# One feed-forward loop, reordered: two tiles' high-weight products first, then the low-weight products of both

## The chip, the cores and the metric

The kernel runs on one core of one Trainium2 chip. The metric is the device time of one launch in microseconds, the median of the runs shown. A core has five engines that run their own instruction streams and meet at semaphores: TensorE (PE) multiplies matrices and writes into eight PSUM banks, VectorE (DVE) and ScalarE (ACT) do elementwise work, GpSimd (POOL) does a little of it and starts transfers, SyncE (SP) starts transfers.

## The reference

Two decoder layers over 256 tokens of width 1024, in float32. Layer 0 mixes with sparse latent attention and stick-breaking attention, layer 1 with block-sparse attention. Behind each mixer stands a normalisation, a feed-forward part and a second normalisation. The change concerns only the feed-forward part:

```
def swiglu(x, w_gate, w_up, w_down):
    return (jax.nn.silu(x @ w_gate) * (x @ w_up)) @ w_down

h = layer_norm(DEEPNORM_ALPHA * h + m, ln_mix_g[i], ln_mix_b[i])
f = swiglu(h, ffn_gate[i], ffn_up[i], ffn_down[i])
h = layer_norm(DEEPNORM_ALPHA * h + f, ln_ffn_g[i], ln_ffn_b[i])
```

The hidden width of the feed-forward part is 2816, that is 22 tiles of 128 columns.

## The kernel before, in words

**Splitting the numbers.** PE multiplies in a shorter format (fp32r). To keep precision each float32 operand is split into a high part (`hi`, the value cast to fp32r) and a low part (`lo`, the rest), and a product is made as hi x hi + hi x lo + lo x hi. Weights arrive as float32 in 1 MB chunks in the buffer `raw` (two slots). ACT casts a chunk to `whi` (`split_hi`, line 376) and DVE subtracts to get `wlo` (`split_lo`, line 753), each in two halves of 128x1024. Both parts lie in the ring `wboth` of six chunks. A chunk is converted four chunks ahead of its use (`AHEAD`). This is the conversion of a chunk in what follows.

**The weight stream.** SP loads the chunks in a fixed order (line 295). It refills a half of a `raw` slot when DVE has done the low half of the chunk that lay there (`wlo_ready`). In the feed-forward loop three chunks make a step: one of `w_down` (two rows of tiles), then two of gate and up (one tile of each).

**PE in a step.** `down` (line 1618) multiplies two finished tiles by their rows of `w_down`: 24 products of 512 columns (line 1244), accumulated in banks 4 to 7 over the whole loop. `gate_up` (line 1607) makes one tile. Its high-weight products (`half_hi`, line 1152) take the high and low parts of the activations side by side as one moving operand of 512 columns: 8 products for gate into one bank, 8 for up into the next; these 16 are a *wide run*. Its low-weight products (`half_lo`, line 1158) have 256 columns and add to the first half of the same banks: 16 products, a *narrow run*. Even tiles use banks 2 and 3, odd ones 0 and 1 (`tile_bank`). Before its wide run a tile waits for its own chunk (`wlo_ready`) and for the sum of the tile two before, which frees the banks (`usum_ready`).

**Evacuation of a tile.** `ffn_tile` on ACT (lines 654 to 661) and on DVE (lines 1050 to 1061) take turns: ACT copies gate's second half out of the bank (L654, when `gate_done` comes from the first half of the narrow run), DVE adds the first half (L1050), ACT applies silu (L657) and copies up's second half (L659, when the tile's last product is done), DVE adds (L1053, this is the sum `usum`) and multiplies (L1058), ACT makes the high part (L661) and DVE the low part (L1061) for `down`.

**The order** is written out by hand on each engine. In `ffn`, two tiles and the start of the first rows stand before the loop; PE runs the first pass of the loop as straight code and three more in a hardware loop. A pass (`four_tiles`) has two steps, so there are eight steps in a layer. `ffn_tile` begins with the conversion of chunk `c + AHEAD`, so ACT's and DVE's order in a step was: conversion, conversion, evacuation, conversion, evacuation. Behind the loop come two single tiles, then the last three down chunks (`last_out`), among which the normalisation `norm` begins. `down` of a step uses the tiles of two pairs before.

Of the kernel before, what the change touches and what calls it, by code (L numbers as in the profile page):

```python
# [43 lines left out]
AHEAD = 4  # L44
# [16 lines left out]
def build(nc, x, xT, stream, w_uk, w_uv, kv_norm, ln_rows, consts, out):  # L61
    with ExitStack() as ctx:
# [207 lines left out]
        def tile_bank(t):  # L270

            return 2 * ((t + 1) % 2)
# [100 lines left out]
        def _(act):  # L373
# [273 lines left out]
            def ffn_tile(L, c, t, i=0, more=1, ahi_first=False):  # L647

                n = FT * L + t + 4 * i
                m = n + 1 - 2 * (L + 1)  # L650
                if more and not ahi_first:
                    split_hi(c + AHEAD, i)
                act.wait_ge(gate_done, m)
                nc.scalar.copy(gful[:, t % 2], bank[tile_bank(t)][:, S:2 * S]).then_inc(glo_ready, 1)  # L654
                act.wait_ge(gsum_ready, m)
                act.wait_ge(amul_ready, n - 1)
                nc.scalar.activation(sgate[:, t % 2], gful[:, t % 2], ACT.Silu).then_inc(silu_ready, 1)  # L657
                act.wait_ge(chunk_used, c + 1 + RING * i)
                nc.scalar.copy(uful[:, t % 2], bank[tile_bank(t) + 1][:, S:2 * S]).then_inc(ulo_ready, 1)  # L659
                act.wait_ge(amul_ready, n + 1)  # L660
                nc.scalar.copy(ahi[:, FF_SLOT[t], :], aful[:, t % 2]).then_inc(ahi_ready, 1)  # L661
                if more and ahi_first:
                    split_hi(c + AHEAD, i)

            def ffn(L):


                base = L0_FFN if L == 0 else L1_FFN
                ffn_rows(L, base)
                for t in (2, 3):  # L670
                    ffn_tile(L, base + t, t)
                with act.Fori(0, LOOPS) as i:
                    for j in range(2):
                        c = base + 4 + 3 * j
                        split_hi(c + AHEAD, i)
                        ffn_tile(L, c + 1, 4 + 2 * j, i)
                        ffn_tile(L, c + 2, 5 + 2 * j, i)
                c = base + 4 + RING * LOOPS
                for at in range(3):
                    more = c + at + AHEAD < CHUNKS  # L680
                    if at < 2:
                        ffn_tile(L, c + at, 4 + 4 * LOOPS + at, 0, more, at == 1)
                    elif more:
                        split_hi(c + at + AHEAD)
# [64 lines left out]
        def _(dve):  # L749
# [6 lines left out]
            def split_lo(c, i=0):  # L756

                for j in range(2):
                    split_lo_half(c, j, i)
# [284 lines left out]
            def ffn_tile(L, c, t, i=0, more=1, alo_first=False):  # L1044
                n = FT * L + t + 4 * i
                m = n + 1 - 2 * (L + 1)
                if more and not alo_first:
                    split_lo(c + AHEAD, i)
                dve.wait_ge(glo_ready, m)
                nc.vector.tensor_tensor(gful[:, t % 2], bank[tile_bank(t)][:, 0:S], gful[:, t % 2], ALU.add  # L1050
                                        ).then_inc(gsum_ready, 1)
                dve.wait_ge(ulo_ready, m)
                nc.vector.tensor_tensor(uful[:, t % 2], bank[tile_bank(t) + 1][:, 0:S], uful[:, t % 2], ALU.add  # L1053
                                        ).then_inc(usum_ready, 1)
                dve.wait_ge(silu_ready, n + 1)
                dve.wait_ge(usum_ready, m)
                dve.wait_ge(alo_ready, n - 1)
                nc.vector.tensor_tensor(aful[:, t % 2], sgate[:, t % 2], uful[:, t % 2], ALU.mult  # L1058
                                        ).then_inc(amul_ready, 1)
                dve.wait_ge(ahi_ready, n + 1)  # L1060
                nc.vector.tensor_tensor(alo[:, FF_SLOT[t], :], aful[:, t % 2], ahi[:, FF_SLOT[t], :].bitcast(F32),  # L1061
                                        ALU.subtract).then_inc(alo_ready, 1)
                if more and alo_first:
                    split_lo(c + AHEAD, i)

            def ffn(L):


                base = L0_FFN if L == 0 else L1_FFN
                ffn_rows(L, base)  # L1070
                for t in (2, 3):
                    ffn_tile(L, base + t, t)
                with dve.Fori(0, LOOPS) as i:
                    for j in range(2):
                        c = base + 4 + 3 * j
                        split_lo(c + AHEAD, i)
                        ffn_tile(L, c + 1, 4 + 2 * j, i)
                        ffn_tile(L, c + 2, 5 + 2 * j, i)
                c = base + 4 + RING * LOOPS
                for at in range(3):  # L1080
                    more = c + at + AHEAD < CHUNKS
                    if at < 2:
                        ffn_tile(L, c + at, 4 + 4 * LOOPS + at, 0, more, at == 1)
                    elif more:
                        split_lo(c + at + AHEAD)
# [44 lines left out]
        def _(pe):  # L1130
# [4 lines left out]
            def chunk(c, i=0):  # L1135
                pe.wait_ge(wlo_ready, 2 * c + 2 * RING * i)
# [12 lines left out]
            def half_hi(dst, slot, off):  # L1149

                for k in range(KT):
                    mm(dst[:], whi[:, slot, off + k * P:off + (k + 1) * P],  # L1152
                       hTs[:, k].rearrange("p j s -> p (j s)"), start=(k == 0), stop=False)

            def half_lo(dst, slot, off):

                for k in range(KT):
                    last = mm(dst[:, 0:S], wlo[:, slot, off + k * P:off + (k + 1) * P], hThi[:, k, :],  # L1158
                              start=False, stop=(k == KT - 1))
                return last  # L1160
# [443 lines left out]
                                               aful[:, tile, t * P:(t + 1) * P], ident)  # L1604
                last.then_inc(ff_turned, 1)

            def gate_up(L, c, t, i=0):

                n = FT * L + t + 4 * i
                chunk(c, i)  # L1610

                pe.wait_ge(usum_ready, n - 1 - 2 * (L + 1))
                for half in range(2):
                    half_hi(bank[tile_bank(t) + half], c % RING, half * KT * P)
                half_lo(bank[tile_bank(t)], c % RING, 0).then_inc(gate_done, 1)
                half_lo(bank[tile_bank(t) + 1], c % RING, KT * P).then_inc(chunk_used, 1)

            def down(L, c, p, i=0, start=False):

# [4 lines left out]
            def ffn(L, n):  # L1624
                base = L0_FFN if L == 0 else L1_FFN

                chunk(base + 1)
                two = slice(base % RING, base % RING + 2)
                rows_wide(2 * L + 1, 0, two, bank[0][:], turn=n).then_inc(rows_done, 1)
                rows_wide(2 * L + 1, 1, two, bank[1][:]).then_inc(chunk_used, 2)  # L1630

                def four_tiles(i, first=False):
                    for j in range(2):
                        c = base + 4 + 3 * j
                        down(L, c, j, i, first and j == 0)
                        gate_up(L, c + 1, 4 + 2 * j, i)
                        gate_up(L, c + 2, 5 + 2 * j, i)

                chunk(base + 2)
                for half in range(2):  # L1640
                    half_hi(bank[tile_bank(2) + half], (base + 2) % RING, half * KT * P)
                turn_rows(L, 0)
                turn_rows(L, 1)
                half_lo(bank[tile_bank(2)], (base + 2) % RING, 0).then_inc(gate_done, 1)
                half_lo(bank[tile_bank(2) + 1], (base + 2) % RING, KT * P).then_inc(chunk_used, 1)
                chunk(base + 3)
                for half in range(2):
                    half_hi(bank[tile_bank(3) + half], (base + 3) % RING, half * KT * P)
                half_lo(bank[tile_bank(3)], (base + 3) % RING, 0).then_inc(gate_done, 1)
                half_lo(bank[tile_bank(3) + 1], (base + 3) % RING, KT * P).then_inc(chunk_used, 1)  # L1650
                four_tiles(0, first=True)
                with pe.Fori(1, LOOPS) as i:
                    four_tiles(i)
                c, p = base + 4 + RING * LOOPS, 2 * LOOPS
                gate_up(L, c, 2 * p + 4)
                gate_up(L, c + 1, 2 * p + 5)
                last_out([(c + 2 + j, FF_SLOT[2 * (p + j):2 * (p + j) + 2], FT * L + 2 * (p + j) + 2)
                          for j in range(3)], n + 1)
# [211 lines left out]
```

## Time and profile before

| | us |
|---|---|
| median of three runs | 600.16 |
| the runs | 600.16, 599.16, 2082.43 |
| the profiled execution | 598.94 |
| its span, first to last instruction | 597.2 |
| PE busy / DVE busy / ACT busy | 589.1 / 424.4 / 342.3 |
| mean granted TensorE clock | 0.998 |

The profile's times are those of one execution. The median isn't moved by the third run, which is far out of line. "Busy" of PE counts overlapping products once. The chain of waits is followed back from the last instruction to what released it, so its pieces add up to the span.

### The profile page before, as it was taken

The page shows a single profiled execution, that of the slowest core. Times are in us where ns is not written, and L with a number is a line of the kernel's source. Part 1 is how long each engine was busy: PE and PEld are TensorE (multiplying, and loading weights), DVE is VectorE, ACT ScalarE, POOL GpSimd, SP SyncE. Part 2 cuts the span into 40 slices and gives each one's busy share as a digit, 9 for nine tenths or more (in the row PEclk, how much of TensorE's full clock was granted, in tenths as well). Part 3 has the DMA queues.
Part 4 walks back from the last instruction along what each step waited for, and adds up shares of the span by engine and source line. Part 5 has one row for each costly group of instructions (what it writes and reads, how often), then busy time and mean ns, then how long its engine had stood idle before and what let it go on. Part 6 is the DMA issues. An engine that isn't in the chain of part 4 may idle for free.

```text
span 597.2 us, 9595 instructions
## 1 busy us (share of the span) xinstructions
PE 589.1 (99%) x3354; PEld 505.7 (85%) x3354; DVE 424.4 (71%) x697; ACT 342.3 (57%) x645; POOL 26.6 (4%) x49
## 2 busy tenths in 40 slices
PE   8999999999999999999999999999999999999995
PEld 7988888888888888888888888888888888888885
DVE  4699877876776556655887888768677666665637
ACT  5776986456655544554556767645565555555530
POOL 1111111100000000000010000002000000000000
PEclk9999999999999999999999999999999999999999
DMA  8755437286676565564447543662767655555401
GB/s 309 265 179 194 142 124 245 91 291 202 223 223 207 193 205 181 182 205 140 143 148 270 180 141 117 205 207 80 237 217 234 210 202 165 185 186 189 140 1 70
DMA packets 30112, 109.43 MB, mean 183 GB/s; under 512 B 3376, under 2 KB 3376, under 8 KB 29952
## 3 DMA queue, kind: packets, MB, share of 16 engines
q1 hardware_dynamic: 28368, 102.25, 51.9%
q0 software_dynamic: 1568, 6.23, 3.4%
q10 hardware_dynamic: 144, 0.52, 0.2%
q8 instruction: 21, 0.34, 0.2%
q14 instruction: 11, 0.09, 0.0%
HBM read 107.94 MB, written 1.05 MB: 183 GB/s over the span
## 4 chain that ended last, share of the span: by engine, by line
PE 98%; DMA 1%; DVE 0%; DVEq 0%; issue 0%; ACT 0%; ACTq 0%
PE bank L1244 27%; PE bank L1152 24%; PE bank L1158 13%; PE bank L1694 5%; PE bank L1522 3%; PE bank L1698 3%; PE bank L1145 2%; PE bank L1222 2%; PE bank L1197 2%; PE bank L1198 2%; PE bank L1204 2%; PE bank L1339 1%; PE bank L1350 1%; PE bank L1330 1%; PE bank L1526 1%; PE bank L1501 1%
## 5 line engine op out<-in xcount | busy, mean ns | idle before, releaser
L753 DVE TENSOR_TENSOR wboth<-raw,wboth 128x1024 fp32r<-128x1024 f32 x190 | 225.3, 1223 | 44.5 <-ACT wboth L376 43.6
L376 ACT CAST wboth<-raw 128x1024 fp32r<-128x1024 f32 x190 | 191.2, 1047 | 21.6 <-DMA raw<-stream_in 20.8
L1152 PE MATMUL bank<-hTs,wboth 128*128 128x512 f32 x640 | 152.2, 390 | 0.0
L1244 PE MATMUL bank<-wboth,oThi 128*128 128x512 f32 x468 | 150.1, 392 | 0.0
L1152 PEld LDWEIGHTS bank<-hTs,wboth 128*128 128x128 f32 x640 | 118.8, 188 | 23.7
L1244 PEld LDWEIGHTS bank<-wboth,oThi 128*128 128x128 f32 x468 | 88.0, 188 | 18.3 <-issue 0.7
L1244 PE MATMUL bank<-wboth,oTlo 128*128 128x512 f32 x234 | 91.3, 390 | 0.0
L1158 PEld LDWEIGHTS bank<-hTs,wboth 128*128 128x128 f32 x640 | 81.9, 191 | 3.0
L1158 PE MATMUL bank<-hTs,wboth 128*128 128x256 f32 x640 | 83.2, 283 | 0.0
L1244 PEld LDWEIGHTS bank<-wboth,oTlo 128*128 128x128 f32 x234 | 44.0, 188 | 8.1
L654 ACT COPY kT<-bank 128x256 f32<-128x256 f32 x40 | 14.8, 371 | 58.8 <-PE bank L1158 58.7
L661 ACT CAST oThi<-scratch 128x256 fp32r<-128x256 f32 x40 | 16.3, 406 | 41.1 <-DVE scratch L1058 41.1
L1050 DVE TENSOR_TENSOR kT<-bank,kT 128x256 f32<-128x256 f32 x40 | 16.8, 420 | 31.5 <-ACT kT L654 31.5
L1053 DVE TENSOR_TENSOR kT<-bank,kT 128x256 f32<-128x256 f32 x40 | 17.0, 425 | 30.4 <-ACT kT L659 30.4
L657 ACT ACTIVATE scratch<-kT 128x256 f32<-128x256 f32 x40 | 16.7, 418 | 36.2 <-DVE kT L1050 36.2
L1694 PE MATMUL bank<-hTs,wboth 128*128 128x512 f32 x128 | 32.6, 395 | 0.0
L1061 DVE TENSOR_TENSOR oTlo<-scratch,oThi 128x256 fp32r<-128x256 f32 x40 | 17.0, 425 | 18.9 <-ACT oThi L661 18.9
L1694 PEld LDWEIGHTS bank<-hTs,wboth 128*128 128x128 f32 x128 | 23.0, 189 | 5.1 <-issue 1.0
L1058 DVE TENSOR_TENSOR scratch<-scratch,kT 128x256 f32<-128x256 f32 x40 | 17.0, 426 | 4.4 <-DVE kT L1053 1.5
L1197 PE MATMUL bank<-wboth,hTs 128*128 128x512 f32 x48 | 18.8, 392 | 0.0
L1198 PE MATMUL bank<-wboth,hTs 128*128 128x512 f32 x48 | 18.7, 391 | 0.0
L1698 PEld LDWEIGHTS bank<-hTs,wboth 128*128 128x128 f32 x128 | 17.4, 190 | 1.3
(189 smaller groups left out, 635.1 us busy)
## 6 DMA issues: line engine op xcount, KB each, us to landing
raw<-stream_in SPq DMA_DIRECT2D x190, 512.0 KB, 4.9
qT<-ln_rows_in POOLq DMA_DIRECT2D x8, 512.0 KB, 5.1
kT<-stream_in SPq DMA_DIRECT2D x2, 512.0 KB, 6.2
h<-x_in POOLq DMA_DIRECT2D x1, 1024.0 KB, 5.0
out<-h SPq DMA_DIRECT2D x4, 256.0 KB, 2.1
v<-xT_in ACTq DMA_DIRECT2D x1, 512.0 KB, 5.1
v<-xT_in SPq DMA_DIRECT2D x1, 512.0 KB, 6.6
dist<-consts_in POOLq DMA_DIRECT2D x1, 384.0 KB, 3.5
```

The lines of the kernel that those rows point to most:

```text
L376: nc.scalar.copy(whi[:, c % RING, j * HW:(j + 1) * HW], raw[:, c % RAW, j * HW:(j + 1) * HW]).then_inc(whi_ready, 1)
L753: nc.vector.tensor_tensor(wlo[:, c % RING, cols], raw[:, c % RAW, cols], whi[:, c % RING, cols].bitcast(F32), ALU.subtract).then_inc(wlo_r ...
L1053: nc.vector.tensor_tensor(uful[:, t % 2], bank[tile_bank(t) + 1][:, 0:S], uful[:, t % 2], ALU.add).then_inc(usum_ready, 1)
L1058: nc.vector.tensor_tensor(aful[:, t % 2], sgate[:, t % 2], uful[:, t % 2], ALU.mult).then_inc(amul_ready, 1)
L1152: mm(dst[:], whi[:, slot, off + k * P:off + (k + 1) * P], hTs[:, k].rearrange("p j s -> p (j s)"), start=(k == 0), stop=False)
L1158: last = mm(dst[:, 0:S], wlo[:, slot, off + k * P:off + (k + 1) * P], hThi[:, k, :], start=False, stop=(k == KT - 1))
L1197: mm(dst, hThi[:, k, toks], whi[:, slots, cols], start=(k == 0), stop=False)
L1198: mm(dst, hThi[:, k, toks], wlo[:, slots, cols], start=False, stop=False)
L1244: last = mm(bank[4 + 2 * t + a][:], o[:, kts[j], t * P:(t + 1) * P], w[:, c % RING, j * D + a * 512:j * D + (a + 1) * 512], start=(start a ...
L1522: mm(dst[:], whi[:, c % RING, at + k * P:at + (k + 1) * P], hTs[:, k].rearrange("p j s -> p (j s)"), start=(k == 0), stop=False)
L1694: mm(dst[:], whi[:, c % RING, at + k * P:at + (k + 1) * P], hTs[:, k].rearrange("p j s -> p (j s)"), start=(k == 0), stop=False)
L1698: last = mm(dst[:, 0:S], wlo[:, c % RING, at + k * P:at + (k + 1) * P], hThi[:, k, :], start=False, stop=(k == KT - 1))
```

## The change

On PE the two tiles of a loop step are now made as a pair (`gate_up_pair`): wide run of the first, wide run of the second, then the narrow runs of both. The single tiles before and behind the loop are as before. On ACT and DVE `ffn_tile` is called with `more=0` in the loop, so that it converts nothing; the conversions stand in the loop: two before the evacuations, the third behind both.

```
                     for j in range(2):
                         c = base + 4 + 3 * j
                         split_hi(c + AHEAD, i)
-                        ffn_tile(L, c + 1, 4 + 2 * j, i)
-                        ffn_tile(L, c + 2, 5 + 2 * j, i)
+                        split_hi(c + AHEAD + 1, i)
+                        ffn_tile(L, c + 1, 4 + 2 * j, i, 0)
+                        ffn_tile(L, c + 2, 5 + 2 * j, i, 0)
+                        split_hi(c + AHEAD + 2, i)
...
-            def gate_up(L, c, t, i=0):
+            def tile_hi(L, c, t, i=0):
 
                 n = FT * L + t + 4 * i
                 chunk(c, i)
...
                 pe.wait_ge(usum_ready, n - 1 - 2 * (L + 1))
                 for half in range(2):
                     half_hi(bank[tile_bank(t) + half], c % RING, half * KT * P)
+
+            def tile_lo_part(c, t):
+
                 half_lo(bank[tile_bank(t)], c % RING, 0).then_inc(gate_done, 1)
                 half_lo(bank[tile_bank(t) + 1], c % RING, KT * P).then_inc(chunk_used, 1)
+
+            def gate_up(L, c, t, i=0):
+
+                tile_hi(L, c, t, i)
+                tile_lo_part(c, t)
+
+            def gate_up_pair(L, c, t, i=0):
+
+                for e in range(2):
+                    tile_hi(L, c + e, t + e, i)
+                for e in range(2):
+                    tile_lo_part(c + e, t + e)
...
                         down(L, c, j, i, first and j == 0)
-                        gate_up(L, c + 1, 4 + 2 * j, i)
-                        gate_up(L, c + 2, 5 + 2 * j, i)
+                        gate_up_pair(L, c + 1, 4 + 2 * j, i)
```

DVE's part is the same as ACT's with `split_lo`.

PE, the two tiles of a loop step, before:

```order
L1152 MATMUL bank<-hTs,wboth 128x512 [waits usum_ready,wlo_ready]
L1152 MATMUL bank<-hTs,wboth 128x512 x15
L1158 MATMUL bank<-hTs,wboth 128x256 x16
L1152 MATMUL bank<-hTs,wboth 128x512 [waits usum_ready,wlo_ready]
L1152 MATMUL bank<-hTs,wboth 128x512 x15
L1158 MATMUL bank<-hTs,wboth 128x256 x16
L1244 MATMUL bank<-wboth,oThi 128x512 [waits alo_ready,wlo_ready]
```

and with the change (its lines are four further down in the file):

```order
L1156 MATMUL bank<-hTs,wboth 128x512 [waits usum_ready,wlo_ready]
L1156 MATMUL bank<-hTs,wboth 128x512 x15
L1156 MATMUL bank<-hTs,wboth 128x512 [waits usum_ready,wlo_ready]
L1156 MATMUL bank<-hTs,wboth 128x512 x15
L1162 MATMUL bank<-hTs,wboth 128x256 x32
L1248 MATMUL bank<-wboth,oThi 128x512 [waits alo_ready,wlo_ready]
```

The second wide run, with its two waits, has moved ahead of the first narrow run, and the narrow runs stand together.

ACT, the second step of a loop pass, from its second conversion (L376, `wboth<-raw`) on, before:

```order
L376 CAST wboth<-raw 128x1024 [waits raw_loaded00,chunk_used]
L376 CAST wboth<-raw 128x1024 [waits raw_loaded01]
L654 COPY kT<-bank 128x256 [waits gate_done]
L657 ACTIVATE scratch<-kT 128x256 [waits amul_ready,gsum_ready]
L658 REGISTER_ALU
L659 COPY kT<-bank 128x256 [waits chunk_used]
L660 REGISTER_ALU
L661 CAST oThi<-scratch 128x256 [waits amul_ready]
L382 REGISTER_ALU
L375 REGISTER_ALU [waits chunk_used]
L376 CAST wboth<-raw 128x1024 [waits raw_loaded10]
L376 CAST wboth<-raw 128x1024 [waits raw_loaded11]
```

and what the change does to it behind that evacuation:

```order
 L661 CAST oThi<-scratch 128x256 [waits amul_ready]
+L654 COPY kT<-bank 128x256 [waits gate_done]
+L657 ACTIVATE scratch<-kT 128x256 [waits amul_ready,gsum_ready]
+L658 REGISTER_ALU
+L659 COPY kT<-bank 128x256 [waits chunk_used]
+L660 REGISTER_ALU
+L661 CAST oThi<-scratch 128x256 [waits amul_ready]
 L382 REGISTER_ALU
 L375 REGISTER_ALU [waits chunk_used]
 L376 CAST wboth<-raw 128x1024 [waits raw_loaded10]
 L376 CAST wboth<-raw 128x1024 [waits raw_loaded11]
```

The two halves of the third chunk's conversion now stand behind the second evacuation. The next step opens with two conversions, so three stand in a row.

## Rows read from the trace of the kernel before

**Rows 1.** The page: busy us, share of the span and instructions of each engine.

```profile
PE 589.1 (99%) x3354; PEld 505.7 (85%) x3354; DVE 424.4 (71%) x697; ACT 342.3 (57%) x645; POOL 26.6 (4%) x49
```

**Rows 2.** The page: the chain that ended last, by engine.

```profile
PE 98%; DMA 1%; DVE 0%; DVEq 0%; issue 0%; ACT 0%; ACTq 0%
```

**Rows 3.** Waits of PE over the whole span: line waited for, us, times, longest.

```profile
PE bank L1370 <- POOL zeros L316: 1.4, 1, 1.4
PE bank L1375 <- DMA v<-xT_in: 0.6, 1, 0.6
```

**Rows 4.** Chain of waits, two loop steps of layer 0: start, us, what.

```profile
187.23 5.47 PE bank L1244 x24
192.70 3.63 PE bank L1152 x16
196.32 1.91 PE bank L1158 x16
198.24 3.65 PE bank L1152 x16
...
209.27 3.63 PE bank L1152 x16
```

**Rows 5.** Busy time of each engine in one loop step; clock, DMA share, GB/s.

```profile
187.23:203.80 16.57, 16.57 (x89) 14.35 (x89) 10.30 (x15) 8.62 (x14) 0.00 (x0) 1.00 0.57 190
```

**Rows 6.** Chain of waits early in the program: a long run of 256-column products.

```profile
15.94 5.76 PE bank L1145 x48
```

**Rows 7.** ACT in order of time, one loop step: start, us, line; idle before.

```profile
197.31 0.37 ACT L654 COPY kT<-bank 128x256 f32<-128x256 f32 x1 [4.01 <-PE bank L1158]
...
199.86 0.41 ACT L661 CAST oThi<-scratch 128x256 fp32r<-128x256 f32 x1 [1.01 <-DVE scratch L1058]
...
202.88 0.37 ACT L654 COPY kT<-bank 128x256 f32<-128x256 f32 x1 [0.71 <-PE bank L1158]
...
206.07 3.90 ACT L376 CAST wboth<-raw 128x1024 fp32r<-128x1024 f32 x4
```

**Rows 8.** DVE in order of time, the same step.

```profile
197.72 0.42 DVE L1050 TENSOR_TENSOR kT<-bank,kT 128x256 f32<-128x256 f32 x1 [2.60 <-ACT kT L654]
...
204.69 0.42 DVE L1053 TENSOR_TENSOR kT<-bank,kT 128x256 f32<-128x256 f32 x1 [0.74 <-ACT kT L659]
...
207.16 4.63 DVE L753 TENSOR_TENSOR wboth<-raw,wboth 128x1024 fp32r<-128x1024 f32 x4 [0.63 <-ACT wboth L376]
```

**Rows 9.** DVE in order of time, tile 3 in both layers; then the chain of waits.

```profile
144.78 0.42 DVE L1053 TENSOR_TENSOR kT<-bank,kT 128x256 f32<-128x256 f32 x1 [0.74 <-ACT kT L659]
436.39 0.42 DVE L1053 TENSOR_TENSOR kT<-bank,kT 128x256 f32<-128x256 f32 x1 [0.74 <-ACT kT L659]
...
142.98 3.63 PE bank L1152 x16
...
436.31 3.63 PE bank L1152 x16
```

**Rows 10.** The loads of line 295: us from issue to landing, min, median, max.

```profile
DMA to landing us min/median/max: 3.6/5.0/7.5
```

**Rows 11.** In order of time behind layer 0's loop: ACT, then DVE.

```profile
280.31 0.37 ACT L654 COPY kT<-bank 128x256 f32<-128x256 f32 x1 [2.13 <-PE bank L1158]
...
275.63 0.42 DVE L1050 TENSOR_TENSOR kT<-bank,kT 128x256 f32<-128x256 f32 x1
```

**Rows 12.** DVE in the normalisation behind layer 0's loop.

```profile
288.79 0.68 DVE L827 SCALAR_TENSOR_TENSOR h<-h,bank 128x512 f32<-128x512 f32 x1
...
294.38 0.75 DVE L859 SCALAR_TENSOR_TENSOR h<-h,small,qT 128x512 f32<-128x512 f32 x1
...
298.51 0.69 DVE L827 SCALAR_TENSOR_TENSOR h<-h,bank 128x512 f32<-128x512 f32 x1 [0.92 <-PE bank L1244]
```

**Rows 13.** Chain of waits behind layer 0's loop.

```profile
281.23 15.67 PE bank L1244 x69
...
303.92 0.87 PE bank L1272 x8
```

More of the change, by code:

```diff
@@ L1076, in ffn @@
                         split_lo(c + AHEAD, i)
-                        ffn_tile(L, c + 1, 4 + 2 * j, i)
-                        ffn_tile(L, c + 2, 5 + 2 * j, i)
+                        split_lo(c + AHEAD + 1, i)
+                        ffn_tile(L, c + 1, 4 + 2 * j, i, 0)
+                        ffn_tile(L, c + 2, 5 + 2 * j, i, 0)
+                        split_lo(c + AHEAD + 2, i)
                 c = base + 4 + RING * LOOPS
```

## The prediction

> **What bounds the kernel now.** I read the page's busy shares first: PE is busy for 589.1 of 597.2 us at a granted clock of 0.998 (the 2.4 GHz level), DVE for 71% and ACT for 57% [rows 1]. Busy shares can hide pipelining, so the chain of waits comes second: 98% of it is PE [rows 2]. Third, PE's own waits: two in the whole program, 2.0 us together, both on the first inputs and far from the feed-forward loops [rows 3]. So in the loops no semaphore ever holds PE. The chain over two loop steps shows this: piece follows piece without a hole, down 5.47, wide 3.63, narrow 1.91, wide 3.65, narrow 1.91 us, a step of 16.57 us [rows 4]. In every loop step DVE works 10.3 us and ACT 8.6 of these 16.57 [rows 5]. Here the reader is to see that a new order of PE's products can gain only what one product costs more in one order than in another, and that a new order of the conversions can gain nothing; it can only lose, where one comes so late that PE waits.
>
> **The change on PE.** There are 2 x 8 loop steps (four passes of two steps in each layer). The number and shapes of the products stay. A wide run that follows a down run takes 3.63 us, one that follows a narrow run 3.65 [rows 4]. The second tile's wide run now follows a wide one: I take 3.63, a gain of 0.02 us in each step. The two narrow runs become one of 32. Low end of its price: 2 x 1.91 = 3.82, as now. High end: the long run of 48 narrow products early in the program, 5.76 us or 0.120 each [rows 6], so 32 x 0.120 = 3.84. A step then takes 16.55 to 16.57 us; I take the middle, since both rows are of the same shape and close: 16 x 0.01 = 0.2 us gained, between 0.0 and 0.3.
>
> **New places where PE can wait.** PE asks for three things in a step, and two of them come at other times.
>
> The second wide run starts 1.91 us earlier (3.63 behind the first instead of 5.54). It needs the bank sum (usum) of the tile two before, and its own chunk's low part. In the steady state that sum ended at 205.1 (204.69 + 0.42) [rows 8] for a run that starts 5.54 us behind 209.27 [rows 4], at 214.81, and would now start at 212.90, with the sum about 1 us later (below): over 6 us are left. The tight place is the first step of each layer, where ACT lags behind the loads. In layer 0, tile 3's sum ends at 144.78 + 0.42 = 145.20, and the run that needs it starts at 142.98 + 5.54 = 148.52; with the change at 142.98 + 3.63 = 146.61. The slack shrinks from 3.3 to 1.4 us. In layer 1 the sum ends at 436.81 and the run would start at 436.31 + 3.63 = 439.94: 3.1 us [rows 9]. Cost: nothing; without this cover each us late costs one, once in a layer.
>
> The first tile's bank halves are ready 3.63 us later, since its narrow run stands behind both wide ones. ACT begins an evacuation about 1 us after the narrow run's start (197.31 for 196.32) and takes to 200.27, 2.96 us [rows 4, 7]. With the change the first starts at 200.94 and ends at 203.90. The second, ready at 202.88 as before, starts at 203.90 and ends near 206.9, where it now ends at 206.07: 0.8 us later. The down product uses tiles of two pairs back, a whole step of cover; the next first-tile sum is needed at 209.27 and would end near 203.9, 5.3 us early.
>
> **The conversions.** The second chunk's conversion moves one place forward on paper only: it already stood directly in front of the first evacuation. The third moves from between the evacuations to behind them, and on both engines three conversions now stand in a row, in front of the next first evacuation. On ACT that is six halves of 0.98 us (four take 3.90) [rows 7]; on DVE six of 1.16 (four take 4.63) [rows 8]. The third needs a raw slot that only the first one's low half frees. From ACT's 206.9: first low half done at 206.9 + 1.09 (DVE follows ACT by that much, 207.16 for 206.07) + 1.16 = 209.2, the second at 210.4; the loads land 5.0 us later at the median, 7.5 at most [rows 10], so 214.2 and 215.4; ACT is done at 216.4, DVE at 217.6. The next first evacuation is not ready before 197.31 + 16.57 + 3.63 = 217.5. It just fits: between 0 us of delay and, with a load of 7.5 us, 2.5; and 5.3 us of cover lie behind it on PE. SP, the queue of these loads, waits for DVE's low halves now too, and the third chunk is needed only two steps on. Cost on PE: nothing.
>
> **Behind the last loop step.** Two conversions (the moved one and the next) now stand in front of the second-last evacuation, where there was one. The last evacuation begins at 280.31 [rows 11]; the loop's last tile is ready two single tiles earlier, 2 x 5.56, at 269.2, and its pair's first now 1.91 before that, at 267.3. So the pair is evacuated from 267.3 to 270.2 and on to 273.2; then four halves end on ACT at 277.1 and on DVE at 278.9. Before, the second-last evacuation had DVE's first sum at 275.63 [rows 11]; such a sum is 2.55 us ahead of ACT's end (197.72 to 200.27) [rows 7, 8], so with the change it ends near 278.9 + 2.55 = 281.4, and the last one starts then, about 1.05 us late. The last down chunk needs it at 281.23 + 5.47 = 286.7 [rows 13], and it is there near 284.8: hidden. But in layer 0 DVE goes on with two conversions and enters the normalisation at 288.79 without a pause; that becomes 289.8. DVE idles 0.92 us for PE before 298.51 [rows 12], so 0.92 of the 1.05 are absorbed there and 0.1 us arrives at PE's turn of the second token tile at 303.92 [rows 13]. For the first token tile's turn, DVE is ready at 294.38 + 0.75 + 1.05 = 296.2 [rows 12], still before 281.23 + 15.67 = 296.90 [rows 13]. In layer 1 no conversion follows: nothing. Cost: 0.1 us, between 0 and 2.6 (0.1 and a load of 7.5 us in place of 5.0).
>
> **Sum.** -0.2 + 0.1 = -0.1 us. The profiled execution took 598.94 us (span 597.2 and 1.7 around it); the undisturbed runs shown are 599.16 and 600.16, so the median lies 1.2 above the profile. Forecast: 598.8 for a profiled one, **600.0** for the median. A measurement of this kernel tells about 2% (12 us) from no change.
>
> **Rivals.**
> - *The boundary of layer 0 pays.* For it: the normalisation's chain passes on whatever exceeds its one pause of 0.92 us [rows 12]. Against: it takes one of the longest loads just there, where the median is 5.0 us [rows 10]. Then 600.0 + 2.6 = 602.6 us. Chance 0.08.
> - *Slower: evacuations bunched behind conversions hold PE's banks.* In each step the first evacuation waits for the third conversion's load. It decides from the point at which that evacuation is over 5.3 us late. With 1 us beyond it, 16 x 1 = 16 us: 616 us. For it: the load chain above ends only 1.1 us (ACT) before the evacuation is ready. Against: the lag would have to be five times what the rows give, and DVE works only 10.3 us of a step, ACT 8.6 [rows 5]. Chance 0.04.
>  The Trainium skill speaks against the change here: "Perfetto Trace Analysis", Optimizing Tensor Performance, has independent groups rotate through PSUM banks, so that the evacuation of one overlaps the next group's products; the pair leaves both tiles open at once and their evacuation mostly under the down run. Taken by itself the rule would let PE wait in each step; by the rows above the down run's 5.47 us and the wide one's 3.63 cover it, and no run here has shown the bunched order yet.
> - *A longer wide run speeds up.* 512 columns at 2.4 GHz are 0.213 us, and a product takes 0.227 (3.63 / 16). Were the 16 of the second wide run to fall to it: 16 x 0.014 x 16 = 3.5 us less, 596.5. Against: 24 down products and 16 wide ones already stand in a row at 0.228 and 0.227 [rows 4]. Chance 0.02.
>  The Trainium skill's "TensorE: Matmul & The Clock Gate", Back-to-back issue gap, gives 215.7 ns for 512 columns and even about 131 in a sustained stream; the trace has neither, with 227.
>
> **How the numbers follow.** The forecast has 0.85; its own range is 598.6 to 601.5 (the runs' spread around it). Adding the boundary case, 598.3 to 602.5 leaves about 1 in 10 out. Faster by over 2%: 0.01, since even the best rival gives 0.6%; slower by over 2%: 0.04; within: 0.95.
>
> **What would show it.** In the changed profile: PE's wait list still with two entries; wide pieces of 3.63 twice in a row and then 32 narrow ones of 3.82 to 3.84, steps of 16.55 to 16.57; first evacuations about 8.25 us behind the pair's start; six conversion halves together on ACT, the fifth with an idle time that a load ended; tile 3's sum still before 146.6; the normalisation of layer 0 entered about 1 us later, and the next stage within 0.3 us of where it was. I am wrong if PE shows a wait for a usum or a chunk in the loops, or if narrow products take over 0.120 us in the long run.

## The result and the profile after

The changed kernel takes 602.69 us, the median of eleven runs from 599.68 to 731.49 (the last far out of line and left out of the comparison; the median of the other ten is 602.1), against 598.88 us for the kernel before in eleven runs on the same chip. The ratio is 1.006, with a 95% interval from 1.0044 to 1.0076: 3.8 us slower by the medians. The forecast of 600.0 us with a range to 602.5 missed it. The runs of the changed kernel also lie further apart than those of before, and the profiled one is the slowest but for that outlier: 607.61 us, span 605.8, granted clock 0.991. So its profile shows the loss at full size, 8.6 us of span more than before, and not that of the median run.

The page of the changed kernel, the rows that answer to [rows 1, 2]:

```profile
PE 592.4 (98%) x3354; PEld 508.1 (84%) x3354; DVE 424.4 (70%) x697; ACT 341.5 (56%) x645; POOL 26.6 (4%) x49
...
PE 68%; DMA 11%; DVE 9%; ACT 6%; issue 5%; DVEq 0%; ACTq 0%; SPq 0%
```

The products are the same in number, yet PE is busy 3.3 us longer. The chain is no longer PE's alone: a quarter of it runs over DMA, DVE and ACT. PE's waits (line waited for: us in total, times, longest), which answer to [rows 3]:

```profile
PE bank L1156 <- DVE kT L1055: 4.9, 2, 2.6
PE bank L1374 <- POOL zeros L316: 1.4, 1, 1.4
PE bank L1379 <- DMA v<-xT_in: 0.5, 1, 0.5
PE bank L1607 <- DVE scratch L1036: 0.4, 1, 0.4
```

The first row is new: a wide run waits for a `usum`, twice in the program, once in each layer. The chain of waits over two loop steps and the end of layer 0's loop (start, us, what), against [rows 4, 13]:

```profile
187.60 5.47 PE bank L1248 x24
193.07 7.25 PE bank L1156 x32
200.32 3.83 PE bank L1162 x32
204.16 5.47 PE bank L1248 x24
...
220.71 5.48 PE bank L1248 x24
226.22 1.06 ACT wboth L376
...
228.44 1.23 DVE wboth L755
229.83 6.33 DMA raw<-stream_in
236.19 1.05 ACT wboth L376
...
243.78 1.05 ACT wboth L376
...
247.39 5.09 DMA raw<-stream_in
...
260.08 1.05 ACT wboth L376
...
263.69 5.30 DMA raw<-stream_in
...
272.39 0.44 DVE kT L1055
272.96 5.50 PE bank L1156 x16
...
280.37 3.65 PE bank L1156 x16
...
285.94 15.67 PE bank L1248 x69
```

Read it from above: PE's own step is 16.56 us (187.60 to 204.16), as forecast, and PE never stops in the loop. But followed back from the end, the chain leaves PE at 226.22 and for 47 us goes round the same circle: the third conversion's load, its cast, its subtraction, two evacuations, the next first conversion, which frees the slot for the next load. It comes back to PE at 272.96, where the first single tile behind the loop has waited for the sum of the last pair's first tile. PE in order of time shows that wait in each layer:

```profile
272.96 5.50 PE L1156 MATMUL bank<-hTs,wboth 128*128 128x512 f32 x16 [2.60 <-DVE kT L1055]
...
570.25 5.49 PE L1156 MATMUL bank<-hTs,wboth 128*128 128x512 f32 x16 [2.33 <-DVE kT L1055]
```

Each wait is followed by a wide run of 5.5 us in place of 3.65. The granted clock of the window goes with it (window; PE busy and instructions; granted clock, DMA share, GB/s); `idle` and `idle_filled` below test that it is the cause:

```profile
262.00:269.00 7.00, 7.00 (x43) 1.00 0.67 222
269.00:276.00 7.00, 4.40 (x22) 0.88 0.64 227
```

The account against the profile of before. Layer 0: 0.43 for a loop that starts later (137.94 for 137.51 us), 2.60 of idleness, 1.85 for the slow wide run (5.50 - 3.65; 0.17 of it isn't the clock's, see the last section), less 8 x 0.02 for the pair order, which is 4.7; the stage behind starts at 285.94 where it was 281.23, 4.71 later. Layer 1: 2.33 + 1.84 - 0.16 = 4.0. Together 8.7, and the spans differ by 8.6.

### The profile page after: what moved, and what is told of

Its sections match the earlier page's. It is cut to its first block, busy times and chain, and to the rows that moved or that the text cites. A ratio compares the mean times of both kernels' runs of the same rounds, so it can differ in the third digit from the quotient of the medians.

```text
span 605.8 us, 9595 instructions
## 1 busy us (share of the span) xinstructions
PE 592.4 (98%) x3354; PEld 508.1 (84%) x3354; DVE 424.4 (70%) x697; ACT 341.5 (56%) x645; POOL 26.6 (4%) x49
## 4 chain that ended last, share of the span: by engine, by line
PE 68%; DMA 11%; DVE 9%; ACT 6%; issue 5%; DVEq 0%; ACTq 0%; SPq 0%
PE bank L1248 18%; PE bank L1156 12%; DMA raw<-stream_in 10%; PE bank L1162 6%; PE bank L1712 5%; DVE wboth L755 4%; ACT wboth L376 4%; PE bank L1526 3%; PE bank L1716 3%; PE bank L1149 2%; PE bank L1226 2%; PE bank L1343 1%; DVE kT L1055 1%; PE bank L1354 1%; PE bank L1334 1%
## 5 line engine op out<-in xcount | busy, mean ns | idle before, releaser
L376 ACT CAST wboth<-raw 128x1024 fp32r<-128x1024 f32 x190 | 192.0, 1047 | 78.3 <-DMA raw<-stream_in 78.0
L1162 PE MATMUL bank<-hTs,wboth 128*128 128x256 f32 x640 | 80.7, 283 | 0.0
L661 ACT CAST oThi<-scratch 128x256 fp32r<-128x256 f32 x40 | 16.3, 406 | 41.1 <-DVE scratch L1060 41.1
L1055 DVE TENSOR_TENSOR kT<-bank,kT 128x256 f32<-128x256 f32 x40 | 17.0, 425 | 30.4 <-ACT kT L659 30.4
L368 POOL TENSOR_TENSOR hTs<-v,hTs 128x256 fp32r<-128x256 f32 x12 | 8.5, 735 | 225.8 <-ACT v L446 225.8
L1716 PE MATMUL bank<-hTs,wboth 128*128 128x256 f32 x128 | 17.8, 282 | 0.0
```

The source lines that it names most:

```text
L376: nc.scalar.copy(whi[:, c % RING, j * HW:(j + 1) * HW], raw[:, c % RAW, j * HW:(j + 1) * HW]).then_inc(whi_ready, 1)
L1716: last = mm(dst[:, 0:S], wlo[:, c % RING, at + k * P:at + (k + 1) * P], hThi[:, k, :], start=False, stop=(k == KT - 1))
```

## The experiments

Two theories stood after this. **Ring**: the conversion order closes a circle of two engines, a slot and a load, whose period exceeds PE's step, so the lag of ACT and DVE behind PE grows over the eight steps until PE meets it behind the loop, where no other work of PE stands in between as cover. **Pair**: PE's new order opens all four gate and up banks at once and holds the evacuations back. Each kernel's ratio is to the kernel before on the same chip (598.85 to 598.87 us).

### PE's pair order alone (pe_only)

ACT and DVE as before; PE as changed. ACT's part of the edit (DVE's is the same):

```
                         split_hi(c + AHEAD, i)
-                        split_hi(c + AHEAD + 1, i)
-                        ffn_tile(L, c + 1, 4 + 2 * j, i, 0)
-                        ffn_tile(L, c + 2, 5 + 2 * j, i, 0)
-                        split_hi(c + AHEAD + 2, i)
+                        ffn_tile(L, c + 1, 4 + 2 * j, i)
+                        ffn_tile(L, c + 2, 5 + 2 * j, i)
```

> The change's order on PE (wide, wide, narrow, narrow), but the conversions where they stood before: two in a row, then evacuation, conversion, evacuation. Theory (load cycle): with the change, two evacuations, a conversion, its freed slot's load and the next but one conversion hang on each other and take 17.0 us where PE needs 16.55 for a step; the lag grows over the loop and meets PE at the first tile behind it, which has no down run in front. Here no load lies in the chain, so nothing grows: no PE wait for a bank sum, and only the 16 x 0.02 us are left: 0.3 us faster than before, about 598.6. Rival (the pair itself): the four open banks and the evacuations one behind the other cause the loss: it stays, 601 to 604, with PE waits of 2 us behind each loop.

598.68 us (598.48 to 599.05, 11 runs), ratio 0.9996 [0.9987, 1.0005]. All of PE's waits, then a step of its chain:

```profile
PE bank L1370 <- POOL zeros L316: 1.4, 1, 1.4
```

```profile
187.21 5.47 PE bank L1244 x24
192.68 7.25 PE bank L1152 x32
...
203.77 5.47 PE bank L1244 x24
```

The one wait left is at the program's start, and a step takes 16.56 us. The pair order costs nothing, and its gain of 0.2 us is too small to be told from nothing. No version here that keeps all of the work is measurably faster than the kernel before.

### The conversion order alone (conv_only)

```
-                        gate_up_pair(L, c + 1, 4 + 2 * j, i)
+                        gate_up(L, c + 1, 4 + 2 * j, i)
+                        gate_up(L, c + 2, 5 + 2 * j, i)
```

> The change's order of conversions on ACT and DVE, but PE as before (wide, narrow, wide, narrow). Theory (load cycle): the same 17 us cycle, so ACT idles some 2.5 us for each half of the third conversion and its evacuations fall behind step by step; but the first tile of a pair is ready 3.6 us earlier and so has 4.4 us instead of 0.8 in front of the first tile behind the loop: little or nothing on PE, 0 to 2 us slower than before (599 to 601). Rival (the pair itself is at fault): no lag and no loss, 598.9. Rival (conversions alone are at fault, whatever PE does): the whole loss, 602 to 603.

600.46 us (599.12 to 606.88, 12 runs), ratio 1.004 [1.0019, 1.0061]: a part of the loss, 1.6 of 3.8 us by the medians and 0.4 of 0.6% by the ratios, and the wide spread come with the conversions alone; the rest needs both parts together. In its profiled execution (599.88 us) PE waits for such a sum once, in layer 1:

```profile
564.13 3.91 PE L1156 MATMUL bank<-hTs,wboth 128*128 128x512 f32 x16 [0.85 <-DVE kT L1055]
```

The lag is there with PE's old order too. ACT's four first conversion halves, in the loop's second step in layer 1 and six turns later:

```profile
449.38 3.89 ACT L376 CAST wboth<-raw 128x1024 fp32r<-128x1024 f32 x4
...
550.71 3.89 ACT L376 CAST wboth<-raw 128x1024 fp32r<-128x1024 f32 x4
```

That is 16.89 us for a turn, where PE's step is 16.57. But the last pair's first tile can be evacuated 3.6 us earlier when its narrow run isn't held back, so there is more cover, and less is lost than with both parts together. The pair order is harmless by itself but spends this cover; that step is worked out from the two orders, not measured on its own.

### A down chunk ahead of the single tiles (down_first)

One of the last three down chunks is multiplied before the first single tile, as cover behind the loop (the counting of the chunk's release moves with it).

```
+                chunk(c + 2)
+                pe.wait_ge(alo_ready, FT * L + 2 * p + 2)
+                for t in range(2):
+                    for a in range(2):
+                        out_part(c + 2, FF_SLOT[2 * p:2 * p + 2], t, a)
                 gate_up(L, c, 2 * p + 4)
...
-                          for j in range(3)], n + 1)
+                          for j in range(1, 3)], n + 1, both=c + 3)
```

> The change whole, and behind each loop the first of the last three down chunks is multiplied ahead of the two single tiles instead of behind them. Theory (uncovered tile): the first single tile now has 5.47 us of down products in front of its wide run, as inside the loop; the lag of up to 3.4 us is covered and PE waits there no more. The last tile's low part may come 0 to 1 us late for the last down chunk. In all 598.6 to 600.5. Rival (the loss is spread over the loop, or lies in the next stage): it stays, 601 to 604.

604.91 us (603.89 to 605.12, 4 runs), ratio 1.0095 [1.008, 1.0109]: slower, a miss of the expectation. PE's waits, then the chain behind layer 0's loop:

```profile
PE bank L1276 <- DVE h L861: 2.9, 2, 2.0
...
PE bank L1248 <- DVE wboth L755: 0.8, 1, 0.8
```

```profile
269.89 5.47 PE bank L1248 x24
...
289.48 4.63 DVE wboth L755 x4
...
299.62 0.76 DVE h L861
```

The wait for the sum is gone, as the ring says. Only layer 1 tests this; in layer 0 the sum was in time even without the cover. In layer 1 it ended at 568.91 us, 2.3 behind the last narrow run's end (566.65), and PE did the down run meanwhile:

```profile
568.49 0.42 DVE L1055 TENSOR_TENSOR kT<-bank,kT 128x256 f32<-128x256 f32 x1 [0.74 <-ACT kT L659]
```

But in layer 0 the single tiles, their evacuations, two conversions and the normalisation all come over 5 us later (the normalisation's first row starts at 294.03 us, where it was 288.79 [rows 12]), and the normalisation's result, not PE, now sets the next turn: the second comes at 307.24 us for 303.92 [rows 13], 3.3 of the 5.9 us that the span grew by. The rest falls in layer 1, behind the wait for the down chunk (0.8) and in the last normalisation, to which the chain goes over at 588.6 us. The cover was taken from a chain that had only 0.92 us to give [rows 12].

### Smaller loads (small_loads)

The changed kernel; in the loops each load brings only a quarter of its half, 128 KB in place of 512 KB. Three quarters of those weights are left out, so the kernel's output is wrong; the instructions of PE, ACT and DVE are all there.

```
-                            sp.dma_start(raw[:, s, half[j]], stream[RAW * i + s][:, half[j]]
+                            part = slice(j * HW, j * HW + HW // 4)
+                            sp.dma_start(raw[:, s, part], stream[RAW * i + s][:, part]
```

> The change whole, but SP's two load loops fetch only the first quarter of each half chunk (128 KB instead of 512 KB), so the weights used there are wrong in part; all instructions of ACT, DVE and PE are the same. Theory (load cycle): a load lands 1.5 us or more earlier, the cycle falls below 16.55 us, the lag never builds up, no PE wait: 598.6. Rival (ACT and DVE work itself, or the clock, makes the lag): the loss stays, 601 to 604.

598.44 us (598.21 to 598.62, 11 runs), ratio 0.999 [0.9982, 0.9999]. PE waits for no bank. Its loads, then ACT in one step (start, us, what; idle before):

```profile
DMA to landing us min/median/max: 2.2/2.3/5.1
```

```profile
190.01 3.90 ACT L377 CAST wboth<-raw 128x1024 fp32r<-128x1024 f32 x4
...
200.77 0.37 ACT L655 COPY kT<-bank 128x256 f32<-128x256 f32 x1 [3.76 <-PE bank L1163]
```

With loads that land in 2.3 us ACT waits 3.8 us for PE again. The same order of instructions with a faster load costs nothing: the load is a necessary part of the loss, as the ring has it and the pair theory does not.

### Half of the steps (early_only, late_only)

The moved conversion in the first four or in the last four steps of each layer; in the others the third conversion stands between the evacuations, as before.

```
+                for lo_i, hi_i in ((0, LOOPS // 2), (LOOPS // 2, LOOPS)):
+                    moved_behind = (lo_i, hi_i) == (0, LOOPS // 2)
...
+                            if not moved_behind:
+                                split_hi(c + AHEAD + 2, i)
+                            ffn_tile(L, c + 2, 5 + 2 * j, i, 0)
+                            if moved_behind:
+                                split_hi(c + AHEAD + 2, i)
```

That is the first kernel; the second has the other half of the range in `moved_behind`.

> PE as in the change; the third conversion behind both evacuations in the first two passes of each loop (steps 1 to 4), between them again in the last two (steps 5 to 8). Theory (the lag grows over the steps and is paid only at the first tile behind the loop): the lag of the first four steps, some 2 us, is worked off in the last four, where ACT has several us of idle time per step; no PE wait for a bank sum, 598.7. Rival (each changed step costs something by itself): half the loss stays, 600.5 to 601.

> PE as in the change; the third conversion behind both evacuations only in the last two passes (steps 5 to 8). Theory (growing lag): four steps give four times 0.45 us less the 1 us or so of air in the first, so about 1 us at the end of the loop, against 0.8 us of cover: PE waits 0 to 1 us in a layer, time 598.7 to 600.5, less than half of the whole loss though half of the steps are changed and they are the ones beside the end. Rival (only the last step's order matters, nothing grows): the whole loss, 602 to 603. Rival (each changed step costs by itself): 600.5 to 601, as with the first half.

Early: 598.6 us (598.39 to 599.54, 11 runs), ratio 0.9997 [0.9988, 1.0006]. Late: 599.38 us (598.5 to 603.44, 11 runs), ratio 1.0019 [1.0005, 1.0034]. By the times, lag from the first four steps is worked off before PE meets it. The early profile had hardly any to work off (207.06 - 157.26 = 49.80 us for three turns, for 49.66 of PE), so it doesn't show this. Four steps at the end build up only a part of the lag, and not in every run (the profiled execution, 598.58 us, has no such wait). Four late steps cost 0.5 us, all eight 3.8, or 4.7 on this same chip (next run): the loss is not a fixed price for each step, and not that of the last step alone.

### The changed kernel once more (after_again)

> The changed kernel once more (an empty line added), for its spread and a second profile beside the others of this chip. Both theories: 601.5 to 603.5 at the median. By the load cycle the time of an execution goes with the landing times of its loads, so the runs spread over more than 2 us where those of before spread over 1, and a profile with a smaller loss has a shorter wait behind the loops, and a wide run behind it that is less slow.

603.55 us (598.81 to 607.52, 6 runs), ratio 1.0093 [1.0067, 1.012]. Its profiled execution happens to be the fastest, 598.81 us with a span of 597.0, and so shows the other end. ACT, the four first conversion halves of some steps; then DVE and the chain at the end of the loop:

```profile
190.44 3.90 ACT L377 CAST wboth<-raw 128x1024 fp32r<-128x1024 f32 x4
207.87 3.90 ACT L377 CAST wboth<-raw 128x1024 fp32r<-128x1024 f32 x4
...
273.37 3.90 ACT L377 CAST wboth<-raw 128x1024 fp32r<-128x1024 f32 x4
```

```profile
269.17 0.43 DVE L1056 TENSOR_TENSOR kT<-bank,kT 128x256 f32<-128x256 f32 x1 [0.74 <-ACT kT L660]
```

```profile
266.06 3.83 PE bank L1163 x32
269.88 3.73 PE bank L1157 x16
```

From 157.17 to 273.37 us are seven steps of 16.60 on the mean, though a single one takes 17.43. The sum ends at 269.60, 0.28 us before PE asks for it. In the first profile of the changed kernel these starts lie 17.01 us apart:

```profile
157.54 3.89 ACT L376 CAST wboth<-raw 128x1024 fp32r<-128x1024 f32 x4
...
209.17 3.90 ACT L376 CAST wboth<-raw 128x1024 fp32r<-128x1024 f32 x4
...
276.60 3.89 ACT L376 CAST wboth<-raw 128x1024 fp32r<-128x1024 f32 x4
```

One program, one order; 0.4 us in each step goes with the difference between 598.8 and 607.6 us.

### Filling PE in front of the single tile (fill)

The changed kernel with 12 products of zero weights ahead of the first single tile.

```
+                for k in range(12):
+                    mm(bank[4 + k % 4][:], zeros[:, 2 * P:3 * P], hTs[:, k % KT].rearrange("p j s -> p (j s)"),
+                       start=False, stop=False, skip_group_check=True)
                 gate_up(L, c, 2 * p + 4)
```

> The change whole, with 12 products of 512 columns by a weight tile of zeros, added to the down banks (which they leave as they are) between the last pair and the first single tile of each layer: 2.7 us of work where PE idled 2.6 and 2.3 us in the changed kernel's profile. Theory (the idle time drops the granted clock, and the wide run behind it then takes 5.5 us for 3.65): no idle time over 1 us, the run back at 3.65 us, clock 0.998 there, and the profiled execution about 604, that is 2 x 2.7 - 0.3 over before. Rival (the run is slow for another reason, as banks read by ACT and DVE at that time): it still takes 5.5 us, and the time is 607 to 608.

One run, 604.0 us (span 602.2), no wait for a bank. ACT's lag happened to be small in it (its last such group starts at 272.89 us), so there was little to fill (in layer 1 the sum ended 0.7 us behind the last narrow run, in layer 0 before it) and it adds its 2 x 2.75 us. Inconclusive on the clock; hence the next pair.

### A fixed wait, bare and filled (idle, idle_filled)

pe_only, which has no lag, with a wait set on purpose before the first single tile; the second kernel has the same 12 products ahead of it.

```
+                pe.wait_ge(wlo_ready, 2 * (c + 3) - 1)
                 gate_up(L, c, 2 * p + 4)
```

> The changed order on PE with the conversions where they stood before (no lag, 598.7), and ahead of the first single tile behind each loop PE waits for the first low half of the chunk converted between the last pair's evacuations: about 2.4 us of idle time in each layer, as long as the changed kernel's profile shows, but with the bank sums long there. Theory (idle time of that length drops the granted clock, and the next wide run pays): a wide run of some 5.5 us behind it, and 598.7 + 2 x (2.4 + 1.8) = 607. Rival (the slow wide run comes from late banks or the engines that read them): 3.65 us and 598.7 + 2 x 2.4 = 603.5.

> The same with 12 products of 512 columns by a weight tile of zeros, added to the down banks, in front of that wait: 2.7 us of PE work in place of the idle time. Theory (clock): no idle time, wide run 3.65 us, 598.7 + 2 x 2.7 = 604.1, some 3 us faster than with the idle time though PE does more. Rival: the same 604.1, but then slower than with the idle time (603.5).

Bare: 606.8 us (605.24 to 607.06, 4 runs), ratio 1.0124 [1.0107, 1.0141]. Filled: 603.88 us (603.82 to 604.21, 4 runs), ratio 1.0085 [1.0068, 1.0102]. PE in the bare one, a window of it, and the same window of the filled one:

```profile
272.23 5.54 PE L1152 MATMUL bank<-hTs,wboth 128*128 128x512 f32 x16 [2.37 <-DVE wboth L753]
```

```profile
269.00:276.00 7.00, 4.63 (x19) 0.80 0.59 196
```

```profile
269.00:276.00 7.00, 7.00 (x35) 1.00 0.58 200
```

Filled, the time is lower by 2.9 us although PE does 2 x 12 products more and starts the tile later: 2.75 us of products take the place of 2.37 us of idleness, which costs 2 x 0.38 = 0.8, and twice 5.54 - 3.65 = 1.9 us come back. That is 3.0, and 2.9 were measured. The second part of the loss, the slow wide run, is the price of the idleness before it and not of the tile.

## Why the prediction was wrong

**The step that failed** is "The conversions ... It just fits ... and 5.3 us of cover lie behind it on PE ... Cost on PE: nothing." It took a delay that repeats for one that happens once. Its parts one by one:

- *Worked out for one step, while the delay is passed on.* The chain above gives the circle's period in three turns: 3.61 us from the four halves' start to the freed slot's load (226.22 to 229.83), the load, and 7.59 from the cast to the next four halves (236.19 to 243.78). With loads of 6.33, 5.09 and 5.30 us that makes 17.6, 16.3 and 16.5, as the starts show (17.56, 16.30, 16.52). So the period is 11.2 us and the load; it stays below PE's 16.55 only up to a load of 5.35. The prediction used 5.0, the median of all loads [rows 10]: a margin of 0.35 us, where it named the 7.5 as a single delay of 2.5. Over six turns in this profile the sum is 102.54 us (157.54 to 260.08) against 6 x 16.55 = 99.30: 3.24 us of lag. Loads of the median would have left none: from 173.99 to 276.60 a turn took 17.10, so the load in the circle took 5.9 on the mean.
- *The cover was that of another place.* 5.3 us stand in front of a pair, where a down run is in between. The first single tile follows the last narrow runs directly. Its banks' sum comes at best 1 us behind the narrow runs' start and 2.0 us of evacuation later, of 3.83: 0.8 us of cover. 3.24 less 0.8 is 2.4, and PE idled 2.60.
- *The price of a wait.* The prediction had each us late cost one. It costs more: 2.60 us of idleness cost another 1.85, all but 0.17 of it by the clock.

**Luck in the number.** The working gives 598.8; the 600.0 came from the median of three runs, taken 1.2 us above the profile. Eleven runs of the kernel before have their median at 598.88. So 1.2 us of the forecast were scatter of the base, and they brought it nearer to the result than its mechanism does, which says no loss where 3.8 us were lost.

Of the rivals, "evacuations bunched behind conversions" named the mechanism, a first evacuation that waits for the third conversion's load, but set it in each step and behind a threshold of 5.3 us, and so asked for five times the lag of its rows. The boundary rival landed near the measured time with another cause: the normalisation of layer 0 began 1.2 us later in `after_again`'s profile, which has no such wait (289.98 for 288.79; 1.0 was worked out), and PE's turns of 296.77 and 303.79 us show none of it.

**What held.** The pair order: 7.25 and 3.83 us, a step of 16.55 to 16.56, no bank wait inside the loops. The Trainium skill's "Perfetto Trace Analysis", Optimizing Tensor Performance, has groups rotate through banks so that one is evacuated while the next is multiplied; pe_only, with four banks open at once, shows no loss (0.9996), since the down run stands in the place of the next group. Tile 3's sum was there at 145.68 in the first profile, 1.4 us before PE asked at 143.41 + 3.63. Neither the fast-product rival nor a price over 0.120 us for a narrow product appeared.

**What stays open.** Why the second half's load lands in 5.1 us in one turn and in 6.3 in the next: the four halves of two slots are asked for within a few us, and the lag differs from run to run. And the median run was not the one profiled. Its mean granted clock was 0.999, as was that of a run of conv_only with 603.49 us, while the traces with two slow wide runs have 0.991 and 0.994. So these runs seem to have lost their 4 us or so by waits alone, without the slow wide runs. In which layer PE waited, and why the clock held, no trace shows. What the ring's other parts are worth (a third slot, a faster conversion) was not tried either.

## What to carry to other kernels

When conversions or other consumers are reordered around a slot buffer, add up the whole circle (free the slot, load, convert, what stands between, free the next) and compare its period with the loop's step; a circle a few tenths longer is invisible in one step and arrives as one wait after eight. Look for the place where the covering work is missing, here behind the loop, and not only at the loop's body. With a margin of 0.35 us against a load that varies by more than that, forecast a spread, not a zero.

## What the runs showed of the hardware

A pause of PE cost more than itself. In PE's order of time an undisturbed run of 16 wide products shows 3.82 us, 0.17 of them under the next run, so 3.65 from one start to the next:

```profile
280.21 3.82 PE L1156 MATMUL bank<-hTs,wboth 128*128 128x512 f32 x16
```

After 2.33 to 2.60 us of idleness (three rows above) it took 5.49 to 5.54 us, and the granted clock of the 7 us window fell to 0.80 to 0.88. The clock accounts for 1.7 us of each, the lost overlap for 0.17. Cut finer, the clock of the changed kernel is 1.00 through the idle time and the first us of products, and falls to 0.50, the 1.2 GHz level, only then:

```profile
275.00:276.00 1.00, 1.00 (x4) 0.50 0.08 33
```

After 0.85 us of idleness (conv_only) the run took 3.91, 0.09 over the undisturbed, and the clock stayed at 1.00:

```profile
562.00:569.00 7.00, 6.14 (x37) 1.00 0.42 156
```
